# Five stage changes in a two-block transformer on one core: opening tile by tile, weight halves round the last square, weights' low parts on VectorE, the key stage's banks and table, and the last sums

## The reference, cut to what matters

```python
def first_block(x, ...):                       # x: 1 x 512 x 1024
    h = rmsnorm(x, pre_mix_g)
    z = einsum('btd,dc->btc', h, w_in)         # 1024 x 3584
    mix = concat(hgrn2_mixer(...), gate_b * causal_dwconv(gate_c * conv_h))
    x = x + rmsnorm(mix @ w_out, post_mix_g)
    u = causal_dwconv(rmsnorm(x, pre_ffn_g) @ ffn_w_up)
    x = x + rmsnorm((silu(gate) * val) @ ffn_w_down, post_ffn_g)
    return x

def second_block(h, ...):                      # two layers
    for l in range(2):
        h = h + 0.5 * swiglu(rmsnorm(h), ...)              # FFN 1, FFN 3
        u = rmsnorm(h)
        h = h + (pool_mixer(u) if l == 0 else mla_attention(u, k_nope, k_rope, v))
        h = h + 0.5 * swiglu(rmsnorm(h), ...)              # FFN 2, FFN 4
        if l == 0:
            kv_a = rmsnorm(h) @ w_dkv          # 128 latent columns, 64 of rotated keys
            k_nope, k_rope, v = ...            # rotated by a table of angles
    return rmsnorm(h, final_norm)
```

## Time and profile before

| What | Value |
|---|---|
| median of 3 runs | 2398.97 us |
| the profiled execution's own time | 2398.69 us |
| its span, first to last record | 2396.7 us |
| TensorE busy | 2334.8 us (97%) |
| VectorE, ScalarE, GpSimd busy | 1671.9, 1005.2, 888.4 us |
| mean granted clock of TensorE | 0.991 of 2.4 GHz |
| HBM read, mean | 90 GB/s |

### The profile page before, as it was taken

The page is one execution under the profiler, slowest core; times in us unless marked ns, Lnnn a source line. Parts: engine busy times, 40 slices in busy tenths (PEclk is TensorE's granted clock), DMA queues, the critical chain, the costliest instruction groups (busy, mean ns, idle before and its releaser), DMA issues. The chain is left out here.

```text
span 2396.7 us, 33477 instructions
## 1 busy us (share of the span) xinstructions
PE 2334.8 (97%) x13500; PEld 2022.0 (84%) x13500; DVE 1671.9 (70%) x1627; ACT 1005.2 (42%) x1259; POOL 888.4 (37%) x461
## 2 busy tenths in 40 slices
PE   7999889999989999999999999999999999999998
PEld 5889677788869999989999979999967778799997
DVE  5688578774279696768786768786777743596874
ACT  4323343432254353454353454353443342443443
POOL 1220322121147355437454336454321101383551
PEclk8999999999999999999999999999999999999999
DMA  4222222222313333223333233323320113223322
GB/s 146 79 71 71 70 71 97 95 88 97 96 62 115 106 106 106 89 71 108 121 94 100 88 106 98 123 94 101 106 58 22 35 53 105 88 86 109 124 84 84
DMA packets 217695, 217.14 MB, mean 91 GB/s; under 512 B 10593, under 2 KB 215008, under 8 KB 217568
## 3 DMA queue, kind: packets, MB, share of 16 engines
q1 hardware_dynamic: 217024, 215.14, 28.4%
q10 hardware_dynamic: 544, 0.20, 0.0%
HBM read 213.22 MB, written 2.10 MB: 90 GB/s over the span
## 5 line engine op out<-in xcount | busy, mean ns | idle before, releaser
L1234 PE MATMUL bank<-Xhi,wlo 128*128 128x256 f32 x1152 | 321.3, 279 | 0.0
L1235 PE MATMUL bank<-Xlo,whi 128*128 128x256 f32 x1152 | 321.2, 279 | 0.0
L1236 PE MATMUL bank<-Xhi,whi 128*128 128x256 f32 x1152 | 321.2, 279 | 0.0
L631 POOL TENSOR_TENSOR sums<-raw 128x512 f32<-128x512 f32 x72 | 144.1, 2001 | 429.8 <-DMA raw<-in_ffn_post_wg_dram 161.6
L933 ACT ACTIVATE whi<-raw 128x2048 fp32r<-128x2048 f32 x72 | 138.2, 1920 | 370.4 <-PE bank L1242 242.0
L1240 PE MATMUL bank<-xghi,wlo 128*128 128x512 f32 x624 | 248.9, 399 | 28.0 <-DVE xglo L1874 22.2
L746 ACT ACTIVATE whi<-raw 128x2048 fp32r<-128x2048 f32 x74 | 141.2, 1907 | 249.9 <-PE bank L1242 235.9
L1242 PE MATMUL bank<-xghi,whi 128*128 128x512 f32 x624 | 245.1, 393 | 0.0
L1863 DVE TENSOR_TENSOR wlo<-raw,whi 128x2048 fp32r<-128x2048 f32 x57 | 131.7, 2310 | 160.3 <-ACT whi L746 160.1
L1234 PE MATMUL bank<-Xhi,sxlo 128*128 128x256 f32 x864 | 242.1, 280 | 0.3
L1236 PE MATMUL bank<-Xhi,sxhi 128*128 128x256 f32 x864 | 240.9, 279 | 0.0
(11 more groups left out here) (356 smaller groups left out, 6077.5 us busy)
## 6 DMA issues: line engine op xcount, KB each, us to landing
raw<-in_ffn_w_up_dram SPq DMA_DIRECT2D x22, 1024.0 KB, 5.1
raw<-in_ffn_pre_wg_dram SPq DMA_DIRECT2D x22, 1024.0 KB, 5.3
raw<-in_ffn_pre_wu_dram SPq DMA_DIRECT2D x22, 1024.0 KB, 5.3
raw<-in_ffn_post_wg_dram SPq DMA_DIRECT2D x22, 1024.0 KB, 5.4
raw<-in_ffn_post_wu_dram SPq DMA_DIRECT2D x22, 1024.0 KB, 5.4
raw<-in_ffn_pre_wd_dram SPq DMA_DIRECT2D x24, 768.0 KB, 4.4
raw<-in_ffn_post_wd_dram SPq DMA_DIRECT2D x24, 768.0 KB, 4.4
raw<-in_w_in_dram SPq DMA_DIRECT2D x14, 1024.0 KB, 5.0
```

The lines of the kernel that those rows point to most:

```text
L631: nc.gpsimd.tensor_tensor(s1, a21, a22, ALU.add).then_inc(adds_done[h], 1)
L1234: nc.tensor.matmul(bank, wl, x, start=first, stop=False, skip_group_check=True)
L1235: nc.tensor.matmul(bank, w, xl, start=False, stop=False, skip_group_check=True)
L1236: return nc.tensor.matmul(bank, w, x, start=False, stop=last, skip_group_check=True)
```

## The change

1. **Opening.** The load of unit 0 is cut into four DMAs of two row tiles each, and its whi and wlo into four pieces of 512 columns. VectorE mixes copies of x, weight pieces and low parts; ScalarE mixes in the same way, with the squares of tiles 2 to 7 behind all high parts. TensorE does both groups of unit 0 tile by tile, then the first group of unit 1, then the sums and vectors, then the second group. The low part of unit 2 goes before the turned vectors on VectorE.
2. **Seams behind w_out and down0.** The next stage's second unit is split in two halves: whi on ScalarE before and after the last square, wlo on VectorE (1024 columns each) and no longer on GpSimd. `project` for w_out is unrolled on ScalarE and VectorE.
3. **Attention's start.** GpSimd's two splits move to VectorE, and both low parts of w_dq's groups come behind the second taking.
4. **Key stage.** w_dkv uses banks 2 and 3; FFN 3 and FFN 4 wait for fewer takings before their first unit, and for all before the second (in all four FFNs). The table of angles is loaded behind the first two units of FFN 3.
5. **End.** The small matmuls on acc go before the turning of the last tile; the last row of ob is scaled half by each engine.

```diff
@@ SyncE: w_in, FFN 3, outputs
-                    load(2 * j + u, u, [(slot(raw, u), win[:, :, c0:c0 + UC])])
+                    if j == u == 0:
+                        for p in range(4):
+                            part_of = slice(2 * p, 2 * p + 2)
+                            sp.dma_start(slot(raw, 0)[:, part_of, :], win[:, part_of, c0:c0 + UC]
+                                         ).then_inc(first_part[p] if p < 3 else raw_ready[0], 16)
+                    else:
+                        load(2 * j + u, u, [(slot(raw, u), win[:, :, c0:c0 + UC])])
...
-            sp.wait_ge(down_done, group_no(3, 0, 0))
-            sp.dma_start(rope_kv[:, :], A["rope"]).then_inc(rope_kv_loaded, 16)
-            ffn(3)
+            def load_rope_kv():
+
+                sp.wait_ge(down_done, group_no(3, 0, 0))
+                sp.dma_start(rope_kv[:, :], A["rope"]).then_inc(rope_kv_loaded, 16)
+
+            ffn(3, load_rope_kv)
...
@@ GpSimd: sum_squares, attention
-                if splits:
-                    split_lo(splits[1], 1)
...
-            pool.wait_ge(whi_ready[0], split_count(UB["attn"], 0))
-            c = slice(1024, UNIT)
-            nc.gpsimd.tensor_tensor(wlo[:, c], raw[:, c], whi[:, c].bitcast(F32), ALU.subtract
-                                    ).then_inc(wlo_ready[0], 4)
-            rope_lo(UB["attn"] + 1)
...
@@ ScalarE: opening, project
+            def half_hi(n, s, part, signal, value):
+
+                a.wait_ge(raw_ready[s], (n - s) * 8 + 16)
+                a.wait_ge(signal, value)
+                c = slice(s * UNIT + part * UNIT // 2, s * UNIT + (part + 1) * UNIT // 2)
+                nc.scalar.activation(whi[:, c], raw[:, c], ACT.Copy).then_inc(whi_ready[s], 2)
...
-            split_hi(0, 0)
+            first_weights(0)
             a.wait_ge(first_gain, 1)
             for k in range(DT):
+                if k in (2, 4, 6):
+                    first_weights(k // 2)
+                if k == 7:
+                    split_hi(1, 1)
                 xg_hi(evacuated, k + 1, xT, "pre_mix_g", k)
+                if k in (4, 5):
+                    square("pre_mix", k - 4, xT)
+            for k in range(2, DT):
                 square("pre_mix", k, xT)
-            split_hi(1, 1)
+            split_hi(2, 0, groups_done, GB["w_in"] + 2)
...
+                        at_seam = seam and (i, b) == (1, 1)
                         for f in range(2):
+                            if at_seam and f:
+                                half_hi(UB[name] + 4 * nk + 1, 1, 0, groups_done, GB[name] + 8)
...
-                        ahead(nk - 1)
+                        if at_seam:
+                            half_hi(UB[name] + 4 * nk + 1, 1, 1, groups_done, GB[name] + 8)
+                        else:
+                            ahead(nk - 1)
...
@@ TensorE: opening, last_down, ffn, narrow
-            up_unit(0, 0, g, "w_in")
-            sum_norm("pre_mix")
-            turn_vectors()
-            up_unit(1, 1, g + 2, "w_in")
+            for k in range(DT):
+                pe.wait_ge(xg_ready, XG["w_in"] + k + 1)
+                pe.wait_ge(wlo_ready[0], k // 2 + 1)
+                for f in range(2):
...
+                if f == 0:
+                    sum_norm("pre_mix")
+                    turn_vectors()
...
+                        if h:
+                            pe.wait_ge(evacuated, GB[{1: "pool", 2: "kv", 3: "dq", 4: "x_out"}[m]])
...
+                pe.wait_ge(acc_added, ADDED["final"] + ADDS["final"])
+                pe.wait_ge(rows_taken, 3)
+                for c in range(TC):
+                    nc.tensor.matmul(banks[2][:, c:c + 1], acc[:, c * P:(c + 1) * P], ones[:, 0:1],
+                                     start=(c == 0), stop=False, skip_group_check=True)
                 turn_rows(7)
...
-                pe.wait_ge(evacuated, GB[{1: "pool", 2: "kv", 3: "dq", 4: "x_out"}[m]])
+                pe.wait_ge(evacuated, GB[{1: "pool", 2: "kv", 3: "dq", 4: "x_out"}[m]] - (0, 0, 0, 4, 2)[m])
...
-            narrow("kv", "kv_pre1", (2, 2))
-            pe.wait_ge(evacuated, GB["kv"] + 4)
+            narrow("kv", "kv_pre1", (2, 2), 2)
...
@@ VectorE: project, attention, end
+                        elif i == 1:
+                            for part in range(2):
+                                half_lo(UB[name] + 4 * nk + 1, 1, part)
...
-                latent_lo(1 + u)
+            latent_lo(1)
+            latent_lo(2)
+            for s, n, c in ((0, UB["attn"], slice(1024, UNIT)), (1, UB["attn"] + 1, slice(UNIT, UNIT + 512))):
+                v.wait_ge(whi_ready[s], split_count(n, s))
+                nc.vector.tensor_tensor(wlo[:, c], raw[:, c], whi[:, c].bitcast(F32), ALU.subtract
+                                        ).then_inc(wlo_ready[s], 4)
```

More of the change, by code:

```diff
@@ L279, in build @@
         first_gain = sem("first_gain")
+        first_part = [sem(f"first_part{p}") for p in range(3)]
         rows_loaded = sem("rows_loaded")
@@ L516, in ffn @@
                         load(up_no(m, i, 1), 1, [(slot(raw, 1), val[:, :, i * UC:(i + 1) * UC])])
+                        if i == 0 and between:
+                            between()
                     k0 = 2 * PAIR0[c]
@@ L661, in last_splits @@
             def last_splits(name, nk):
-                return [UB[name] + 2 * nk * (i + 1) + 1 for i in range(2)]
+                return [UB[name] + 2 * nk + 1]
             sum_squares("pre_mix")
@@ L842, in _, with project @@
                     nc.scalar.activation(tile(xghi, h - 1), tile(CH, h - 1), ACT.Copy).then_inc(xghi_ready, 1)
-            def project(name, ksplit, norm, unroll=False, t=xT, limit=UNITS, after=None):
+            def project(name, ksplit, norm, unroll=False, t=xT, limit=UNITS, after=None, seam=False):
                 nk = len(ksplit)
@@ L923, in _ @@
             up(0, "pre_ffn", conv=True)
-            project("down0", DOWN, "post_ffn", unroll=True, t=None)
+            project("down0", DOWN, "post_ffn", unroll=True, t=None, seam=True)
             def fill_up(m, i, h, part, signal, value):
@@ L1345, in _ @@
             pe.wait_ge(ones_ready, 2)
-            up_unit(0, 0, g, "w_in")
-            sum_norm("pre_mix")
-            turn_vectors()
-            up_unit(1, 1, g + 2, "w_in")
+            for k in range(DT):
+                pe.wait_ge(xg_ready, XG["w_in"] + k + 1)
+                pe.wait_ge(wlo_ready[0], k // 2 + 1)
+                for f in range(2):
+                    if k == 0:
+                        pe.wait_ge(evacuated, f + 1)
+                    m = three(ring[f][:, :], slot(whi, 0)[:, k, f * P:(f + 1) * P], slot(wlo, 0)[:, k, f * P:(f + 1) * P],
+                              tile(xghi, k), tile(xglo, k), k == 0, k == DT - 1)
+                    if k == DT - 1:
+                        m.then_inc(groups_done, 1)
+            for f in range(2):
+                bank_free(g + 2 + f)
+                for k in range(DT):
+                    if f == 0 and k in (0, 4):
+                        pe.wait_ge(wlo_ready[1], 2 + k // 2)
+                    m = three(ring[2 + f][:, :], slot(whi, 1)[:, k, f * P:(f + 1) * P],
+                              slot(wlo, 1)[:, k, f * P:(f + 1) * P], tile(xghi, k), tile(xglo, k), k == 0, k == DT - 1)
+                m.then_inc(groups_done, 1)
+                if f == 0:
+                    sum_norm("pre_mix")
+                    turn_vectors()
             g += 4
@@ L1689, in narrow @@
                         pe.wait_ge(xg_ready, XG[name] + k + 1)
-                        m = three(ring[u][:, :], w[:, k, :], wl[:, k, :], tile(xghi_kv if name == "kv" else xghi, k),
+                        m = three(ring[bank0 + u][:, :], w[:, k, :], wl[:, k, :], tile(xghi_kv if name == "kv" else xghi, k),
                                   tile(xglo_kv, k),
@@ L1845, in _ @@
             ffn(4, one_by_one, lambda: sum_norm("post1"))
-            pe.wait_ge(acc_added, ADDED["final"] + ADDS["final"])
-            pe.wait_ge(rows_taken, 3)
-            for n, part in enumerate((acc[:, :], sq[:, T:2 * T])):
-                if n:
-                    pe.wait_ge(square_ready, DT * (NORM["final"] + 1))
-                for c in range(TC):
-                    ins = nc.tensor.matmul(banks[2][:, c:c + 1], part[:, c * P:(c + 1) * P], ones[:, 0:1],
-                                           start=(n == 0 and c == 0), stop=(n == 1), skip_group_check=True)
+            pe.wait_ge(square_ready, DT * (NORM["final"] + 1))
+            for c in range(TC):
+                ins = nc.tensor.matmul(banks[2][:, c:c + 1], sq[:, T + c * P:T + (c + 1) * P], ones[:, 0:1],
+                                       start=False, stop=True, skip_group_check=True)
             ins.then_inc(final_sums, 1)
@@ L1890, in _ @@
                 xg_lo("w_in", k, k, tile(xT, k), "pre_mix_g")
-            split_lo(1, 1)
+                if k < DT - 2:
+                    copy_x(k + 2)
+                if k in (0, 2, 4):
+                    first_weights(k // 2 + 1)
```

(10 more changed lines are left out.)

53 lines of the change are left out of this document (35 added, 18 removed).

## The result

The changed kernel takes 2378.14 us (median of 4 runs, 2377.83 to 2378.98), the kernel before, run beside it, 2398.74 us (2397.63 to 2399.2). The ratio is 0.9915, with a 95% interval of 0.9904 to 0.9926: faster, by 20.6 us. The prediction said 2377.0 us and 2373.8 to 2381.5. The profiled execution took 2377.91 us with a span of 2376.1 us.

What follows compares the result with a forecast made beforehand. TensorE bounds it, busy 2334.8 of 2396.7 us, so only its pauses can shrink; 7.1 + 3.6 + 3.55 + 4.8 + 2.05 + 0.6 = 21.7 us off 2398.69 gives 2377.0 us, range 2373.8 to 2381.5.

Steps and rivals of the forecast that it cites:

- Opening: Kernel start: first matmul at 13.6 us instead of 19.84, unit 1 ending at 45.2 instead of 52.3; 7.1 us gained.
- the prediction's other reckoning, by the lock: Opening: wlo halves each keep a GpSimd addition waiting throughout, sums start 0.6 us later, gain 6.5 us.
- I keep the dip behind them: Opening: 3.4 us at 1.2 GHz behind the sums and turned vectors stays, costing 1.6 us.
- rival B: Opening: dip behind the sums stays away (2375.4 us), or the clock rises only at 24.0 (2378.9 us); 15%.
- Seams: Behind w_out and down0: earlier Ln and a first product no longer held by GpSimd; 3.6 and 3.55 us gained.
- 0.4 + 3.2: Seam behind w_out: 0.4 us from whi split in two, 3.2 us from VectorE's halves replacing GpSimd's low part.
- FFN 3: Start of FFN 3: the 3.2 us wait for the key rotation's bank and the following 1.6 us dip go; 4.8 us.
- Attention: Attention's start: the taking for keys(1) no longer stands behind a low part slowed beside GpSimd; 2.05 us gained.
- so the gain passes through: After both seams: later tiles go at VectorE's pace or wait for its chain, so each seam's gain reaches the end.
- C: Seams: products slow for a reason of their own, not GpSimd's; 6.4 us missing there, about 1.5 in attention; 2385 us; 5%.
- D: A new wait: an FFN 3 tile or the opening's sums 2 to 3 us late from VectorE's added work; 2380 us; 8%.
- E: Opening: short pauses between tiles keep the clock at 1.2 GHz; slower than before once held 47 us; 2%.

Runs made afterwards that it cites:

- G1: The kernel before with w_out unrolled and 14 idle waits ahead on VectorE, putting up0's loop at place 274; 2401.73 us, ratio 1.0015.
- E4: Changed kernel with opening's sums before both unit 1 groups, w_dkv in banks 0 and 1, attention's low part before the taking, acc matmuls last; 2392.03 us.
- E2: Changed kernel with the low part of up0's odd units moved from GpSimd to VectorE; 2368.0 us, ratio 0.9871.
- F2: Changed kernel with 12 idle waits ahead on VectorE, putting up0's loop at place 280; 2375.61 us, ratio 0.9901.
- E3: Changed kernel: low part whole on GpSimd behind w_out, high part whole behind down0, angle table before weights, attention's splits on GpSimd; 2380.48 us, ratio 0.9923.
- E1: The kernel before with only the loops of w_out on ScalarE and VectorE unrolled; 2397.81 us, ratio 0.9996.

## Why the prediction was right, and where not

- **Opening (7.1, measured 8.4).** The path was as worked out: 13.74 for 13.6, high clock from 17.7 for 17.5, 33.5 for 33.5. The wait for the sums is 0.94 us and not 0.5, because five additions take 9.18 us (8.4 forecast) beside VectorE's two halves, which together take 4.54 us and which I had put at 1.2 each. So the sums start at 34.42 for 34.0: 0.4 us of the 0.6 that the prediction's other reckoning, by the lock, had given. Two sums of the prediction are off by a little: 34.0 + 3.9 + 5.45 + 1.6 is 44.95 and not 45.2, so that its terms give 7.35 us; and its upper bound, without the dip and the wait, is 9.2 and not 8.7. The step that failed is "I keep the dip behind them" (1.6 us). That is rival B, and the runs show that it is no property of either kernel: with the old opening the stretch at 1.2 GHz at about 41 us is there in three traces of four and missing in G1; with the new one (E4 left out) it is missing in five of six and there in E2, with nothing changed ahead of it.

```profile
41.00:44.30 3.30, 3.30 (x16) 2.73 (x15) 3.00 (x3) 0.73 (x1) 0.00 (x0) 1.00 0.00 0
```

  That is G1, and this E2:

```profile
38.70:42.00 3.30, 3.30 (x9) 2.63 (x8) 2.17 (x6) 0.00 (x0) 0.00 (x0) 0.50 0.96 312
```

  E2 and F2 also have no slow stretch at all at the opening's start, where the changed kernel has one from 14.3 to 17.7. E2's traced execution, the one with the dip, is also the slowest of its four (2370.32 us, the others 2367.34 to 2368.35). So 1.6 us of the profiled 8.4 can't be counted on, and the traced gain without them is 6.8; whether the new opening makes the dip rarer, ten traces don't tell. The Trainium skill's sentence on this (TensorE: Matmul & The Clock Gate, What's actually happening: the watch does not start with the kernel) agrees with these traces.
- **Seams (3.6 and 3.55; 3.64 each).** Right, mechanism and size. Only the split 0.4 + 3.2 doesn't stand: the first part alone gives 0.85 and the second 2.1, each tested at one seam only.
- **FFN 3 (4.8; 4.93).** Right, and the dip went with the pause, as it came back with it in E4. Not needed are the earlier weights, with which the prediction had reckoned: in E3 the banks alone do it, with 0.3 us to spare.
- **Attention (2.05; 2.0).** Right, mechanism and size: the low part L2449, held by GpSimd, stood in front of the taking. What the runs add is that the change removes this twice: either remedy alone suffices (E3, E4).
- **End (0.6; 0.6).** Right; E4 gives 0.7 for the matmuls alone.
- **up0's loop (0; -2.4).** The failed sentence is "so the gain passes through": the sum has no term for this loop. "I cost them at nothing", of the unrolled loops, holds for the unrolling itself (E1), but not for the place to which the change as a whole moves the next loop. In the kernel before this loop already has a held product and pauses of 0.4 us per turn. They are the sign of a loop without slack, in which 0.1 us of VectorE per turn reaches the end, and a tie decides over 0.35 more.
- Rivals: B came in part (no dip). C, D and E did not: no product is slow by itself, no new wait came at the places that D named (a loss of D's size came in up0's loop), and the clock was high from 17.7.

The median gain is 20.6 us, 1.1 less than the forecast 21.7: +1.3 in the opening and small change against -2.4 in the loop. That the total came so close is luck in part, since the dip that stayed away hides two thirds of the loop's loss; with it I estimate 2379.7 us (2378.14 + 1.6), still inside the range.

## What to carry to other kernels

If TensorE pauses in every turn of a loop for another engine, as here for VectorE, that engine has no slack there: before costing an edit elsewhere at nothing, ask what 0.1 us more per turn would do, and remove the hold on that engine first. Here moving one more split off GpSimd was worth 10 us, more than any single part of the change, in a place that the change left alone. If the time moves by a few us where no instruction changed, shift the loop by some idle waits before looking for a cause in the edit. And when several edits serve one pause, undo them one at a time: of the two at FFN 3 one did nothing, of the two at attention either would have done.

## What the runs showed of the hardware that I had not expected

- The place of a loop in an engine's program changed the gap between two dependent instructions from 0.15 to about 0.25 us, in every turn, in four kernels of eleven. In a fifth (E1) the same gap fell on another instruction of the turn and cost nothing.
- Two engines that start within 0.03 us of each other: VectorE's product starts 0.03 us ahead of GpSimd's split both times, at 354.79 it is held all the same for the split's whole length, at 400.50 it gets through. The order of the starts in the trace does not say who has won.
- GpSimd does not hold every VectorE instruction. In E3 a product that reads a PSUM bank and R takes 0.69 us in the middle of GpSimd's 3.39 us, and the next one, with both inputs in SBUF, takes 1.38 and ends 0.55 after it. The Trainium skill (SBUF — State Buffer, section SBUF: two separate sides) says so: of VectorE's instructions like these, the lock takes in those with two SBUF inputs, and whoever starts first has it to the end. The first trace row of E3's attention agrees with the latter: VectorE's 1.22 us starts first, 0.09 us ahead, and is whole, GpSimd's 1024 columns take 3.39 us behind it, where 2048 took 4.50.
